# Tile 0's dots, sums and the modulation placed anew in a two-layer inference step on one core

## What is computed

```python
def trunk_layer(x, cond, p, lambda_init, cache):
    sh1, sc1, g1, sh2, sc2, g2 = jnp.split(jax.nn.silu(cond) @ p['w_mod'] + p['b_mod'], 6, axis=-1)
    mix, ctx = token_mixing(modulate(x, sh1, sc1), p, lambda_init, cache)   # 4 branches, 12 heads
    x = layer_norm_affine(ALPHA * x + g1[:, None] * mix, p['ln1_g'], p['ln1_b'])
    ffn = peer_ffn(modulate(x, sh2, sc2), p['peer_w_q'], p['peer_subkeys'], p['peer_u'], p['peer_v'])
    return layer_norm_affine(ALPHA * x + g2[:, None] * ffn, p['ln2_g'], p['ln2_b']), ctx

# peer_ffn, for each token: 8 heads x 16 chosen of 16384 experts, 128 rows of u and 128 of v
    act = gelu(einsum('td,tkd->tk', xt, take(u_tab, e, axis=0))) * g      # the dots
    out = einsum('tk,tkd->td', act, take(v_tab, e, axis=0))               # the sums
```

## Time and profile before

| what | us |
|---|---|
| median of 3 runs | 3267.99 |
| lowest, highest | 3265.26, 3273.81 |
| the profiled execution | 3269.04 |
| its span, first to last instruction | 3267.2 |
| mean granted TensorE clock | 0.781 |

### The profile page before, as it was taken

How to read it: one execution, slowest core, us unless ns; L and a number is a source line. 1 busy time by engine, 2 the same in 40 slices (tenths; PEclk the granted TensorE clock), 3 DMA queues, 4 the chain that set the end, 5 groups by cost and what they waited for, 6 DMA issues and landing times.

```text
span 3267.2 us, 29211 instructions
## 1 busy us (share of the span) xinstructions
PE 1955.7 (60%) x9808; PEld 1122.2 (34%) x9808; DVE 1771.5 (54%) x4513; ACT 375.9 (12%) x914; POOL 1694.6 (52%) x1540
## 2 busy tenths in 40 slices
PE   7899732989870007656679539698986000233465
PEld 3586511757450002214455114565654000000111
DVE  4532599732339995344531475973125999544400
ACT  1121001221010001011111001232101000000000
POOL 0000376533338666556645627663335766777775
PEclk9889965899995558877889869888998555566677
DMA  8756697878779779999999949896888877999998
GB/s 325 295 182 223 234 377 264 319 264 316 278 259 339 266 262 381 420 418 419 419 419 419 419 178 405 328 362 243 318 292 290 294 260 261 349 420 419 417 419 340
DMA packets 296212, 1070.98 MB, mean 328 GB/s; under 512 B 33537, under 2 KB 36353, under 8 KB 295297
## 3 DMA queue, kind: packets, MB, share of 16 engines
q0 software_dynamic: 221184, 805.40, 65.3%
q1 hardware_dynamic: 71712, 253.16, 20.3%
q10 hardware_dynamic: 3168, 10.55, 0.8%
HBM read 1065.67 MB, written 3.31 MB: 327 GB/s over the span
## 4 chain that ended last, share of the span: by engine, by line
PE 38%; DVE 23%; POOL 14%; DMA 13%; issue 12%; ACT 1%; SPq 0%; DVEq 0%; ACTq 0%; POOLq 0%
PE psum L870 8%; POOL ring L1750 8%; DMA ring<-in_peer_v,v_experts 7%; POOL work L1750 6%; PE psum L780 6%; PE psum L859 5%; DVE ring L1298 5%; PE psum L1029 5%; DMA work<-in_peer_v,v_experts 4%; PE psum L895 3%; PE psum L1011 3%; DVE work L1298 2%; PE psum L821 2%; PE psum L972 1%; DVE work L1477 1%
## 5 line engine op out<-in xcount | busy, mean ns | idle before, releaser
L1750 POOL DMA_INDIRECT ring<-in_peer_u,experts x520 | 640.9, 1233 | 731.9 <-DVE experts L1529 374.1
L1750 POOL DMA_INDIRECT ring<-in_peer_v,v_experts x520 | 512.6, 986 | 542.4 <-PE psum L780 393.9
L780 PE MATMUL psum<-ring,z 128*32 128x512 f32 x2080 | 377.5, 762 | 228.6 <-DMA ring<-in_peer_v,v_experts 175.8
L1298 DVE CUSTOM_DVE_ANT_0 ring<-ring,work 128x1024 f32<-128x1024 f32 x264 | 320.1, 1226 | 143.7 <-DMA ring<-in_peer_u,experts 138.9
L1298 DVE CUSTOM_DVE_ANT_0 work<-work 128x1024 f32<-128x1024 f32 x248 | 299.9, 1225 | 153.2 <-DMA work<-in_peer_u,experts 149.7
L1750 POOL DMA_INDIRECT work<-in_peer_u,experts x248 | 291.3, 1174 | 168.1 <-issue 61.7
L1044 PE MATMUL psum<-consts,work 128*128 128x128 f32 x6 | 2.7, 447 | 626.7 <-DVE experts L1529 626.7
L780 PE MATMUL psum<-work,z 128*32 128x512 f32 x992 | 234.4, 872 | 207.7 <-DMA work<-in_peer_v,v_experts 133.6
L1298 DVE CUSTOM_DVE_ANT_0 ring<-ring,h2a 128x1024 f32<-128x1024 f32 x256 | 305.0, 1223 | 63.3 <-DMA ring<-in_peer_u,experts 61.2
L870 PE MATMUL psum<-work,wring 128*128 128x256 f32 (+1 forms) x1760 | 328.1, 346 | 0.0
L870 PEld LDWEIGHTS psum<-work,wring 128*128 128x128 f32 x1760 | 287.5, 199 | 50.9 <-issue 22.7
(11 more groups left out here) (202 smaller groups left out, 2553.6 us busy)
## 6 DMA issues: line engine op xcount, KB each, us to landing
wring<-in_wpack SPq DMA_DIRECT2D x370, 512.0 KB, 7.1
ring<-in_wpack SPq DMA_DIRECT2D x98, 512.0 KB, 5.9
ring<-in_peer_u,experts POOLq DMA_INDIRECT x520, 6.4
ring<-in_peer_v,v_experts POOLq DMA_INDIRECT x520, 8.0
work<-in_rows ACTq DMA_DIRECT2D x4, 1024.0 KB, 8.0
work<-in_peer_u,experts POOLq DMA_INDIRECT x248, 6.2
work<-in_peer_v,v_experts POOLq DMA_INDIRECT x248, 9.0
wring<-in_wpack SPq DMA_DIRECT2D x16, 160.0 KB, 5.7
```

What stands on the lines that cost most here:

```text
L780: last = nc.tensor.matmul(psum[QUARTER * c:QUARTER * (c + 1), 6 + q, :], z[:, at:at + QUARTER], row(("v", n, o))[:, 512 * q:512 * (q + 1)] ...
L1298: nc.vector.tensor_tensor_reduce(row(key), row(key), h2_of(t), 1.0, 0.0, ALU.mult, ALU.add, dots[:, k:k + 1]).then_inc(dots_ready, 1)
L1750: pool.indirect_dma_start(row(key), None, a["peer_" + what], bass.IndirectOffsetOnAxis(ap=index, axis=0)).then_inc(got[ROW_CELL[key]], 16)
```

## The change

- **Places.** Tile 0's and tile 3's dots lie over 0.6 of the cost (`late`), not half; 24 of their 32 sum steps over the rest up to the choosing of the next tile; six over its first two groups; the last two beside the next tile's dots, which begin only there, followed by the finish. `cost` is changed too: a topk piece from 3 to 1, `mod` from 7 to 5. By these costs the 0.6 of stage 1 falls on (s 1,23,0), its last head, and in stage 3 on (gate 3,2,3).
- **Modulation.** All parts go to PE, with block kk in column group kk % 4, a stationary of 32 columns (two vectors and 30 zeros; `cond` and `silu` are widened) and two blocks added in each group; ACT copies 128x512, and four matmuls with a two-column 0/1 matrix (`sum_up`) turn and add. `macc` is gone from DVE.
- **Evacuation.** `o`, `h2` and `pq` go to ACT. For the scaled heads DVE's reciprocal raises a new semaphore (`sums_turned`), on which ACT waits ahead of the scaled copy.
- **Cells.** The number of ring cells is taken from the last u asked for, so the eight late steps of v may use 21. `experts` holds two tiles by turns, not three.

```diff
-    return {"mod": 7, "modt": 1, "macc": 6, "hT": 1, "proj": 7, "norms": 12 * T, "gate": 1.8 * T, "sgu": 1, "tt": 1,
+    return {"mod": 5, "modt": 1, "hT": 1, "proj": 7, "norms": 12 * T, "gate": 1.8 * T, "sgu": 1, "tt": 1,
             "mq": 2, "kv": 1, "mqt": 1, "mkt": 1, "s": 1.5, "pt": 1, "o": 1, "ot": 1, "br": 0.6 * T, "outs": 8, "gb": 1.5,
-            "mix": 7, "ln1": 9, "h2T": 2, "h2": 1, "pq": 1.8 * T, "ps": 1, "topk": 12 / HEAD_GROUPS}.get(x[0], 0)
+            "mix": 7, "ln1": 9, "h2T": 2, "h2": 1, "pq": 1.8 * T, "ps": 1, "topk": 1}.get(x[0], 0)
...
-        half = part(first, chosen, 0.5)
-        dots = dots_of(n)
+        late = part(first, chosen, 0.6)
+        dots, sums, next_dots = dots_of(n), sums_of(n), dots_of(n + 1)
         if m:
             set_(finish_items(n - 1), PLACE[("begin", 3)])
-        lay(dots[8 * (m > 0):], first, half)
-        set_(turn(n), half + 2)
-        last = PLACE[("topk", m + 1, 0, 2, 0)]
-        lay(sums_list(n, True), half + 3, last)
+        lay(dots[8 * (m > 0):], first, late)
+        set_(turn(n), late + 2)
+        lay(flat(sums[:24]), late + 3, chosen)
+        two = PLACE[("topk", m + 1, 0, 2, 0)]
+        lay(flat(sums[24:30]), chosen, two)
+        lay(beside(next_dots, sums[30:], 6) + finish_items(n), two, PLACE[("begin", 2)] if m == 0 else end)
         if m == 0:
-            one, two = dots_of(1), dots_of(2)
-            lay(one, PLACE[("topk", 1, 0, 1, 2)], PLACE[("begin", 2)])
+            dots = dots_of(2)
...
     for at, key in enumerate(ASKS):
-        c = min(range(RINGS if key[1] in TIGHT else CELLS), key=lambda i: when[i])
+        if key[0] == "u":
+            room = RINGS if key[1] in TIGHT else CELLS
+        c = min(range(room), key=lambda i: when[i])
...
-                                last = nc.tensor.matmul(out[0:2, :], silu[:, kk, :], w[:, k, :], start=(kk == 0), stop=(kk == KD - 1))
+                                c = QUARTER * (kk % 4)
+                                last = nc.tensor.matmul(out[c:c + QUARTER, :], silu[:, kk, :], w[:, k, :], start=(kk < 4), stop=(kk >= 4))
...
-                            pe.wait_ge(macc_ready, j - 3)
...
+                            last = nc.tensor.matmul(out[:, 2 * n:2 * n + 2], v.modacc[:, j % 2, n * P:(n + 1) * P], sum_up, start=True, stop=True)
...
-                        taken(nc.scalar.copy(v.modacc[0:2, it[2] % 2, :], bank(it)[0:2, :]))
+                        taken(nc.scalar.copy(v.modacc[:, it[2] % 2, :], bank(it)))
...
+                    elif kind == "o":
...
+                            act.wait_ge(sums_turned, SOFT_NO[(m, w)])
+                            taken(nc.scalar.activation(v.proj[:, i, c:c + 64], bank(it)[:, 0:64], ACT.Copy, scale=stat[:, 112 + r:113 + r]))
```

More of the change, by code:

```diff
@@ L165, in modt @@
     return ("modt", mod_stage(l), j, l)
-def mod_by_vector(l, j):
-    return l == 0 and 4 <= j < 10
 def mod_items(l, parts):
@@ L175, in mod_items @@
     for n, j in enumerate(parts):
-        if mod_by_vector(l, j):
-            out += [("macc", mod_stage(l), j, k, l) for k in range(2)] + [modt(l, j)]
-        else:
-            out += [("mod", mod_stage(l), j, l)] + ([modt(l, parts[n - 1])] if n else [])
-    return out if mod_by_vector(l, parts[-1]) else out + [modt(l, parts[-1])]
+        out += [("mod", mod_stage(l), j, l)] + ([modt(l, parts[n - 1])] if n else [])
+    return out + [modt(l, parts[-1])]
 def stage_items(m):
@@ L197, in stage_items @@
             if j < 6:
-                out += [("macc", m, 4 + j, k, l) for k in range(2)] if mod_by_vector(l, 4 + j) else [("mod", m, 4 + j, l)]
+                out += [("mod", m, 4 + j, l)]
     out += [("norms", m)] + gates_first(m)
@@ L357, in schedule @@
             middle = part(b, done, 0.6)
-            lay(two[:6] + turn(1) + beside(two[6:], sums_of(1), 6) + finish_items(1), b, middle)
+            lay(dots[:6] + turn(1) + beside(dots[6:], sums_of(1), 6) + finish_items(1), b, middle)
             set_(turn(2), middle + 2)
@@ L362, in schedule @@
         else:
-            lay(dots_of(4), PLACE[("topk", 3, 0, 1, 2)], end)
-            five = dots_of(5)
-            set_(five[:6] + turn(4) + beside(five[6:], sums_of(4), 6) + finish_items(4), end)
+            dots = dots_of(5)
+            set_(dots[:6] + turn(4) + beside(dots[6:], sums_of(4), 6) + finish_items(4), end)
             set_(turn(5) + flat(sums_of(5)) + finish_items(5), end)
     return at
-def sums_list(n, finish):
-    return flat(sums_of(n)) + (finish_items(n) if finish else [])
 def program():
@@ L446, in evacuator @@
     return FIXED_BY[kind]
-NO_PSUM = ("begin", "macc", "norms", "outs", "ln1_rows", "ln1", "topk", "u", "gm", "zf", "v", "fin")
+NO_PSUM = ("begin", "norms", "outs", "ln1_rows", "ln1", "topk", "u", "gm", "zf", "v", "fin")
 ITEMS = [x for x in PROGRAM if x[0] not in NO_PSUM]
@@ L471 @@
         SLOTS += [("mod", _m, _x[3], _x[2], q) for q in range(4)]
-    elif _x[0] == "macc":
-        SLOTS += [("mod", _m, _x[4], _x[2], 2 * _x[3] + q) for q in range(2)]
     elif _x[0] == "proj" and _x[3] == 0:
@@ L505 @@
 for _s in SLOTS:
-    if _s[0] in ("in", "out") or _s[0] == "mod" and not mod_by_vector(_s[2], _s[3]):
+    if _s[0] in ("in", "out", "mod"):
         if _s[-1] < 3:
@@ L515, in last_item @@
     if s[0] == "mod":
-        return ("modt" if mod_by_vector(s[2], s[3]) else "mod", m, s[3], s[2])
+        return ("mod", m, s[3], s[2])
     if s[0] == "in":
@@ L738, in _ @@
                             sp.wait_ge(part_used, PART_NO[before])
-                        elif before[0] == "mod" and mod_by_vector(before[2], before[3]):
-                            sp.wait_ge(macc_ready, before[3] - 3)
                         else:
@@ L825, in _ @@
                         out = room(it)
[L826 to L837 removed]
+                        evacuated(pe, ("mod", m, j, it[3]))
+                        for n in range(4):
+                            last = nc.tensor.matmul(out[:, 2 * n:2 * n + 2], v.modacc[:, j % 2, n * P:(n + 1) * P], sum_up, start=True, stop=True)
                         last.then_inc(psum_full, 1)
@@ L1367, in shift_scale @@
                     taken(last)
-                def mod_products(m, j, half, l):
-                    v = VIEW[m]
-                    if half == 0:
-                        full(dve, modt(l, j - 1))
-                    for k in range(4):
-                        if k % 2 == 0:
-                            n = SLOT_OF[("mod", m, l, j, 2 * half + k // 2)]
-                            dve.wait_ge(w_ready[W_PLACE[n]], 16 * W_USE[n])
-                            w = weights(n, W_SLOT).rearrange("p (k n) -> p k n", k=2)
-                        for c in range(2):
-                            s_ = silu[:, 4 * half + k, c:c + 1]
-                            if half == 0 and k == 0:
-                                ins = nc.vector.tensor_scalar(v.modacc[:, c, :], w[:, k % 2, :], s_, None, ALU.mult)
-                            else:
-                                dve.wait_ge(dve_step, steps[0] - 1)
-                                ins = nc.vector.scalar_tensor_tensor(out=v.modacc[:, c, :], in0=w[:, k % 2, :], scalar=s_,
-                                                                     in1=v.modacc[:, c, :], op0=ALU.mult, op1=ALU.add)
-                            step(ins)
-                    if half == 1:
-                        sync()
-                        dve.sem_inc(macc_ready, 1)
                 def rotate(dst, src, t, groups, half, kc, ks, hold):
```

107 lines of the change are left out of this document (43 added, 64 removed).

## The result

The kernel before took 3270.9 us (median of four runs), the changed kernel 3189.6 us (3186.4 to 3192.4): ratio 0.9753, 95% interval 0.9736 to 0.9771. The forecast was 3190. The profiled execution of the changed kernel is its slowest, 3192.4 us with a span of 3190.5.

The account below looks back on a forecast made before the run. No engine is full over the span; stretches are bound in turn by DVE, PE or DMA. 23 + 48 - 2 - 7 + 11 = 73, plus 5, gives 78 off 3269: 3191, 3190 against the median; range 3150 to 3240.

Parts of the forecast that it names:

- Start: Modulation at the start: four column groups shorten the parts on PE, so the gates begin earlier; gain 23 us.
- The drain at a change of tiling mode: Modulation at the start: switching costs nothing visible; if as long as one record, twelve would take 5 us off the gain.
- First choosing: Tile 0's choosing, 374 to 518 us: 40 fewer dots on DVE, 96 us instead of 144; gain 48 us.
- rival B: Dots saved in the choosing come back in the attention; 3225 us, or 3235 with late v rows; chance 0.12.
- Up to the next choosing: 640 to 947 us: cost 2 for more dots beside the attention, cost 7 for 24 sum steps instead of about 20.
- Layer 1's mixing: 2042 to 2484 us: dots over 0.6 instead of 0.5 of the cost; gain 11 us.
- the evacuation term: Head outputs moved to ScalarE: helps DVE only in stretches counted as 4 us, elsewhere hides under PE or DMA; 0.
- The choosings: 947 to 1240 and 2484 to 2778 us: eight sum steps and the finish move beside DVE-bound choosing; 0, at most 10 each.
- rival D: Choosings of tiles 1 and 4: first u asks queue behind v's on POOL, DVE starves; 3300 us; chance 0.05.
- 1.25 us an ask: POOL in the choosings: 24 v asks ahead of the first u ask take 30 us, the time of two groups.
- Context stage of layer 1 and the tail: DMA-bound 1240 us to the next choosing, and from 2778 on: lengths unchanged; context stage 0, 8 either way.
- Their rate is full: DMA-bound context stage of layer 1: DMA already at share 1.03 and 417 GB/s, so no time changes; 0.

Follow-up runs that it names:

- topk_cost3: Changed kernel with the step cost of a choosing (topk) piece back at 3 instead of 1; 3209.3 us, ratio 0.9807 to the kernel before.
- evac_dve: Changed kernel with `h2` and `pq` evacuations split between VectorE and ScalarE again and `o` back on VectorE; ratio 0.9748 to the kernel before.
- aligned_sums_18: Changed kernel with row cells at multiples of 256 bytes and 18, not 24, sum steps ahead of the next choosing; 3186.9 us, ratio 0.9741 to the kernel before.

## Why the prediction was right

*Start: 23 forecast, 27 to 29 measured.* The gates begin at 119.4, not 124 to 126, where they began at 147.3. The parts end at 31.4 (forecast 31) and the projections begin at 36.4 (34.7): the first four parts are limited by their weights, as said. Behind that two terms were too large: a part is 1.85 us, not the 2.8 taken between the two clocks (6 us), and a turning 0.79, not 1.3 (3 us). The granted clock is 0.98 of 2.4 GHz from 44 to 124, for 0.82 before, when PE stood between parts for DVE's products. The right row was the step at full clock. Turning, part and projection follow without a gap (80.49 + 0.79 = 81.28, 81.28 + 1.85 = 83.13). The drain at a change of tiling mode, which the Trainium skill names (TensorEngine Tiling (Array Packing), Key Properties), costs nothing to be seen in this trace, in which the ends of matmuls are modelled.

*First choosing: 48 forecast, 49 measured,* and 52 with the attention up to gate (1,1,2); it is 95 us for a forecast 96. 37 dots are begun when it ends, where 75 were: 38 fewer, not 40. DVE has 87 of the 95, a little more than the 82 forecast, so it is still at 0.9, which the prediction had said it wouldn't be. 45.0 us of it are 74 records of dots:

```profile
345.00:440.00 95.00, 44.97 (x74) 0.69 0.91 345
440.00:562.00 122.00, 65.73 (x110) 0.79 0.83 302
```

(stretches of the dots' line, L1291, in the changed kernel). The saved dots didn't come back in the attention (111.4 us for 111.0): rival B is out, and `topk_cost3`, which changes one number alone, shows it: of the 31 us that its 24 dots more cost in the choosing, the attention gives back 9, not all.

*Up to the next choosing: cost 9 forecast, 9 measured* (+8.6). The sums alone (L766):

```profile
655.00:874.00 219.00, 48.05 (x368) 10.29 (x360) 0.96 0.88 317
874.00:1166.00 292.00, 26.29 (x144) 5.40 (x136) 0.55 0.90 324
```

24 steps for about 20; the one at the border is counted in the second line. The eight in the choosing cost DVE nothing.

*Layer 1's mixing: 11 forecast, 17 measured.* The places give 7.5, close enough; the rest is mostly the evacuation term, taken at 0 and worth 7.5 by `evac_dve`. The step that failed is "it helps DVE in stretches counted above as 4 us; elsewhere it hides".

*The choosings: 0 forecast, 4 and 7 us gained.* DVE's busy time is the same; it waits less. The first dot of tile 1 stands 33.4 us into the choosing, as forecast, and rival D (POOL's queue starves DVE) didn't come. `aligned_sums_18` shows that it is near: with six steps more in the choosing 14 to 17 us of it come. The prediction's 1.25 us an ask left out the 0.3 us between asks, so POOL had less room there than it counted.

*Context stage of layer 1 and the tail: 0 forecast, 23 us lost.* This is the larger step that failed. "The bytes are the same" holds: 721.8 us at 390 GB/s and 735.1 at 382 are both 281 MB. "Their rate is full" took the rate of before for a constant of the engine. It hangs on where the buffers lie, which the change moved without a line of the diff saying so. With the addresses put right the same kernel would have been at 3167, still within the range of 3150 to 3240, but below my forecast's own 3170.

So that the number 3190 was met to the microsecond is luck: 23 us gained above the forecast stand against 23 lost. Its mechanisms, with the exceptions of the rate and of the evacuations, were there.

## What to carry to other kernels

When a change makes any tile in SBUF wider, look at where the tiles behind it now start. A saturated gather of 4096-byte rows lost 2.4% because its cells moved off multiples of 256 bytes. A stretch that DMA bounds is free cover for work, but it isn't a constant: compare its GB/s, and not its share, before and after.

When work is spread over stretches with different bounds, count for each step every resource that it takes along. A sum step is 2 us of PE, 2 MB of rows and four asks of 1.6 us on POOL; moving six of them out of a mixing that PE bounds gave 12 us there and cost 14 in a choosing where POOL was all but full. And a step that ends a chain, like the finish, takes its waits along: set ahead of the choosing, it held DVE for 15 us.

## What the runs showed of the hardware

- Gathers of 4096-byte rows into cells at a multiple of 256 bytes: 419 GB/s at DMA share 1.03; at 192 bytes past one: 409 GB/s at the same share. In both directions with the same instructions, and so in all 14 profiled executions, on either pair of chips. No other offset was tried.
- 16 matmuls of 128x512 with a 32-column stationary: 1.85 us in four column groups, 6.98 in one. Steps of full width follow at once.
- Four chips ran the same kernel, at 3272, 3273, 3349 and 3355 us. Most of the difference is in the tail of u and v rows (360 for 420 GB/s from 2860 to 3000 us), while both pairs reach 419 in the middle of the run. Its cause is open.
- Asks back to back on POOL beside a busy DVE took 1.3 us each and 0.3 between them, in the changed kernel's choosing, and moved 324 GB/s at DMA share 0.90.
